# High weights meet both parts of the later tokens in one matmul, with token halves of 280 and 240

## The chip, the cores and the metric

The kernel runs on one core of one Trainium2 chip. The metric is the device time of one launch in microseconds; the kernel before takes 1524.72 us, the median of three runs (1524.21 to 1529.47). Engines by their short names: PE is TensorE (PEld its weight loads), DVE is VectorE, ACT is ScalarE, POOL is GpSimd, SP is SyncE, which issues the DMAs here.

## The reference

One inference step of a two-layer decoder over 512 prompt tokens and 8 sample tokens, all in float32: layer 0 mixes with an S5 state-space block, layer 1 with attention that reads one shared K/V; both also attend to 256 memory tokens; both end in a ConvFFN. What matters here is the part that is linear in the tokens:

```python
h = rmsnorm(x, p['norm_mix_pre'][l]);  z = h @ p['w_in'][l]            # (520, 1024) @ (1024, 1024)
...
o = jnp.concatenate([seq_out, mem_out], axis=-1) @ p['w_out'][l]       # 1024 -> 1024
x = x + rmsnorm(o, p['norm_mix_post'][l])
f, cp = conv_ffn(rmsnorm(x, p['norm_ffn_pre'][l]), ...)
x = x + rmsnorm(f, p['norm_ffn_post'][l])

def conv_ffn(h, w_up, cw, cb, w_down, prev):
    u = h @ w_up                                   # 1024 -> 5632
    y, new_prev = causal_dwconv(u, prev, cw, cb)   # width 3 along the tokens
    g, val = jnp.split(y, 2, axis=-1)
    return (jax.nn.silu(g) * val) @ w_down, new_prev   # 2816 -> 1024
```

Between the layers the shared K, V and log-forget values are made from x by `rmsnorm(s, g) @ w_kv` (1024 to 1548).

## The kernel before

Activations lie transposed: features on the 128 partitions, the NT = 520 tokens (512 of the prompt, 8 samples) along the free axis. A dense product is cut into panels of 128 output features. To keep float32 precision with single-pass float32r matmuls, both operands are split: w = w_hi + w_lo, x = x_hi + x_lo, each part rounded to float32r, and three products are added in PSUM, hi·hi, hi·lo and lo·hi. The tokens are cut into HALF = (0, 264) and (264, 520), each in a PSUM bank of its own. So `product` (L2638) does, for each k of a panel (KD = 8 blocks of 128 input features, KH = 11 for half of the "down" product), six matmuls, three terms times two halves, L2649. The memory keys and values use the same function with one range of 256 columns.

**A panel's way through the engines.** Panel q lies in slot q % 2: one of two weight buffers and two of the four banks of `big`. SP loads the raw weights (`raw`). ACT makes w_hi (L2144), for panel q + 2 once panel q is done (`panel_done`). POOL makes w_lo = raw - w_hi (L949; in some phases DVE does, L1208) and raises `lo_made`. PE waits for `lo_made` and, before it writes a slot's banks again, for `panel_read` of the panel two before (L2640 to L2642). DVE waits for `panel_done`, reads both banks and raises `panel_read` with the second read.

**Who reads.** `read_panel` (L1549) serves w_in of layer 0 and K/V: it multiplies each half by rstd, the token's inverse norm, on the way out of PSUM. The queries of layer 1 are read on L1944 to L1950. w_out and "down" are copied or added into y by `copy_out` (L1776 to L1796), `read_half` (L1762) and the loop at L1857 to L1860. Of the last pair of panels of such a phase PE does the first half of both panels and then the second half of both (`last_pair`, L2704); `first_pair` (L2732) starts a phase in the same way.

**The "up" panels.** The FFN is done in two halves of the hidden width, f = 0 and 1; each has 22 "up" panels (11 pairs: a gate panel and its value panel) and then 8 "down" panels over KH = 11 blocks. With two layers that is 4 phases of 11 laps. DVE's lap is the loop at L1809. For each of the two panels: two reads with the factor rstd into `uc` (L1826 and L1827, the second raises `panel_read`); a wait for ACT's tap, in which ACT first copies the last tokens (`newconv`, L2502, it waits for `panel_read`) and then scales `uc` into `yc` (L2506); then two scalar_tensor_tensor over 512 tokens that add the taps before (L1831, L1836), each with a small one for the 8 samples (L1834, L1837). After the second panel: hf = silu(gate) * value, h_hi and h_lo (L1842 to L1846), which the "down" product takes as its right side. All of these from L1831 on read and write SBUF.

DVE and ACT run their queues in the order written; nothing is scheduled at run time.

Of the kernel before, what the change touches and what calls it, by code (L numbers as in the profile page):

```python
# [21 lines left out]
F32R = mybir.dt.float32r  # L22
# [6 lines left out]
P = 128  # L29
T = 512  # L30
NB = 8
NT = T + NB
HALF = ((0, 264), (264, NT))
# [268 lines left out]
def program(nc, I, O):  # L302
# [4 lines left out]
    with ctx:  # L307
# [63 lines left out]
        x_hi = split("x_hi", [P, KD, NT], F32R)  # L371
        x_lo = split("x_lo", [P, KD, NT], F32R)
# [82 lines left out]
        h_hi = a("h_hi", [P, KH, NT], F32R)  # L455
        h_lo = a("h_lo", [P, KH, NT], F32R)
# [725 lines left out]
        def _(dve):  # L1182
# [366 lines left out]
            def read_panel(q, dst_of, mult=True):  # L1549
# [212 lines left out]
            def read_half(ph, m, n, add):  # L1762
# [7 lines left out]
                ins = V.tensor_tensor(dst, dst, src, add) if add else V.tensor_copy(dst, src)  # L1770
# [5 lines left out]
            def copy_out(ph, add=None, conv=None):  # L1776

                for m in range(6):
                    q = PH[ph][2] + m
                    dve.wait_ge(panel_done, q + 1)  # L1780
                    for n_, (c0, c1) in enumerate(HALF):
                        dst, src = y[:, m, c0:c1], big[2 * (q % 2) + n_][:, 0:c1 - c0]
                        ins = V.tensor_tensor(dst, dst, src, add) if add else V.tensor_copy(dst, src)
                        if n_:
                            tell(ins, panel_read, q + 1)
                        else:
                            do(ins)
# [10 lines left out]
            def ffn(l):  # L1798
                for f in range(2):
                    _, n, base, _ = PH[f"up{l}{f}"]  # L1800
                    step0, r = own.n, None
                    K = 10
# [6 lines left out]
                    with dve.Fori(0, KH) as it:  # L1809
# [6 lines left out]
                        def sy():  # L1816
                            dve.wait_ge(dve_step, it * K + (step0 + c[0]))

                        for half in range(2):
# [6 lines left out]
                            st(V.tensor_tensor(uu[:, 2:266], big[2 * slot][:, 0:264], rstd[:, 0:264], ALU.mult))  # L1826
# [1592 lines left out]
```

## Time and profile before

| | |
|---|---|
| median of three runs | 1524.72 us (1524.21 to 1529.47) |
| span of the profiled execution, first to last instruction | 1519.0 us |
| PE busy | 1413.4 us, 93% |
| PEld busy | 1313.9 us, 86% |
| DVE busy | 976.7 us, 64% |
| POOL busy | 638.5 us, 42% |
| ACT busy | 576.7 us, 38% |
| mean granted TensorE clock | 0.971 |

The page gives the profiled execution no time of its own beside the span; the runs' median is 5.7 us above it. Busy time is the union of an engine's instructions. A matmul's record is longer than the distance to the next one, since matmuls overlap in the array: the cost of one in a stream is the distance between two starts. A row of the timeline gives start, duration, engine, line, operation, out<-in, shapes, and in brackets how long the engine was idle before and what ended that. The chain of work is followed back from the last instruction.

### The profile page before, as it was taken

The numbers are of one execution on the slowest core, as the hardware profiler recorded it, in microseconds if no ns is written. First come the engines' busy times: TensorE is split into PE (matmuls) and PEld (weight loads), VectorE is DVE, ScalarE is ACT, GpSimd is POOL, SyncE is SP. The second block draws the span as 40 slices with busy tenths as digits, with TensorE's granted clock in tenths as the row PEclk, the third lists the DMA queues.
The fourth block names the chain that finished last, engine by engine and source line by source line (L and its number), as shares of the span: only waits on it lengthen the run. The fifth ranks groups of instructions, "written<-read, shape, count | busy, mean of one in ns | idle before, by whom it ended". The sixth has DMA issues, their size and how long they took to land.

```text
span 1519.0 us, 32537 instructions
## 1 busy us (share of the span) xinstructions
PE 1413.4 (93%) x12097; PEld 1313.9 (86%) x12097; DVE 976.7 (64%) x1658; ACT 576.7 (38%) x1019; POOL 638.5 (42%) x420
## 2 busy tenths in 40 slices
PE   6986978989999999999799989999989999999997
PEld 6984758979999999999699966657889999999997
DVE  5769967576773167765748688753677761376755
ACT  4544354344432133422415235432454431234323
POOL 1586422304444334433177888402223443344430
PEclk9998789989999999999999999999999999999999
DMA  5344364213333232332145769995213233233321
GB/s 173 114 117 79 63 169 123 83 44 85 99 94 98 77 97 83 102 98 75 45 121 164 226 175 308 331 340 157 69 57 97 84 103 90 83 91 88 104 83 62
DMA packets 289082, 180.47 MB, mean 119 GB/s; under 512 B 54248, under 2 KB 274572, under 8 KB 288924
## 3 DMA queue, kind: packets, MB, share of 16 engines
q1 hardware_dynamic: 288412, 179.07, 40.9%
q8 instruction: 61, 1.00, 0.3%
q14 instruction: 33, 0.27, 0.1%
q10 hardware_dynamic: 576, 0.13, 0.0%
HBM read 167.10 MB, written 10.63 MB: 117 GB/s over the span
## 4 chain that ended last, share of the span: by engine, by line
PE 70%; DVE 14%; issue 8%; ACT 2%; SPq 2%; DMA 1%; POOL 1%; DVEq 0%; ACTq 0%; POOLq 0%
PE big L2649 58%; PE big L2715 3%; PE misc L2800 2%; DVE tmp L1261 2%; PE big L2746 2%; DVE y L1738 1%; DVE rstd L1219 1%; DVE x L1744 1%; DVE w_lo L1208 1%; DVE x_lo L1251 1%; SPq L597 1%; PE misc L2770 1%; ACT yc L2506 1%; DVE cp L1261 1%; ACT w_hi L2144 1%
## 5 line engine op out<-in xcount | busy, mean ns | idle before, releaser
L949 POOL TENSOR_TENSOR w_lo<-raw,w_hi 128x1024 fp32r<-128x1024 f32 (+2 forms) x153 | 393.8, 2574 | 708.9 <-ACT w_hi L2144 548.4
L2144 ACT ACTIVATE w_hi<-raw 128x1024 fp32r<-128x1024 f32 (+2 forms) x179 | 198.5, 1109 | 582.1 <-PE big L2649 539.0
L2649 PE MATMUL big<-x_hi,w_hi 128*128 128x264 f32 x1984 | 406.7, 287 | 8.4 <-DVE uc L1827 2.8
L2649 PE MATMUL big<-x_hi,w_lo 128*128 128x264 f32 x1984 | 400.8, 283 | 0.0
L2649 PE MATMUL big<-x_lo,w_hi 128*128 128x264 f32 x1984 | 398.8, 283 | 0.0
L2649 PEld LDWEIGHTS big<-x_hi,w_hi 128*128 128x128 f32 x1984 | 305.9, 189 | 13.1 <-issue 4.7
L2649 PEld LDWEIGHTS big<-x_lo,w_hi 128*128 128x128 f32 x1984 | 305.6, 189 | 0.0
L2649 PEld LDWEIGHTS big<-x_hi,w_lo 128*128 128x128 f32 x1984 | 305.3, 189 | 0.0
L1831 DVE SCALAR_TENSOR_TENSOR yc<-uc,convw,yc 128x512 f32<-128x512 f32 x88 | 136.7, 1554 | 113.2 <-ACT yc L2506 113.2
L2649 PE MATMUL big<-h_hi,w_hi 128*128 128x264 f32 x616 | 125.1, 284 | 6.3 <-DVE h_lo L1846 6.3
L2649 PE MATMUL big<-h_hi,w_lo 128*128 128x264 f32 x616 | 123.9, 282 | 0.0
L2649 PE MATMUL big<-h_lo,w_hi 128*128 128x264 f32 x616 | 123.9, 282 | 0.0
L2649 PEld LDWEIGHTS big<-h_hi,w_hi 128*128 128x128 f32 x616 | 94.1, 188 | 7.4 <-DVE h_lo L1846 7.1
L2649 PEld LDWEIGHTS big<-h_lo,w_hi 128*128 128x128 f32 x616 | 94.4, 188 | 0.0
L2649 PEld LDWEIGHTS big<-h_hi,w_lo 128*128 128x128 f32 x616 | 94.4, 188 | 0.0
L1859 DVE COPY y<-big 128x264 f32 (+1 forms) x32 | 12.2, 424 | 102.6 <-PE big L2649 102.6
L1093 POOL TENSOR_TENSOR areas<-areas,qb 128x768 f32<-128x768 f32 x41 | 74.6, 1830 | 7.0 <-DMA areas<-in_cache_k 6.2
L1836 DVE SCALAR_TENSOR_TENSOR yc<-uc,convw,yc 128x512 f32<-128x512 f32 x88 | 66.2, 752 | 12.7 <-DVE yc L1834 0.2
L2506 ACT ACTIVATE yc<-uc,convw 128x520 f32<-128x520 f32 x88 | 72.3, 821 | 1.1
L1201 DVE TENSOR_TENSOR sumsq<-sumsq,sq 128x520 f32<-128x520 f32 x20 | 52.5, 2627 | 11.7 <-ACT sq L2461 9.9
L2746 PE MATMUL big<-x_hi,w_hi 128*128 128x264 f32 (+1 forms) x96 | 38.4, 400 | 17.8 <-DVE x_lo L1251 10.4
L1219 DVE RECIPROCAL rstd<-sd 128x264 f32<-128x264 f32 (+1 forms) x16 | 28.3, 1773 | 31.5 <-ACT sd L2177 31.5
(434 smaller groups left out, 2330.8 us busy)
## 6 DMA issues: line engine op xcount, KB each, us to landing
raw<-in_w_up SPq DMA_DIRECT2D x88, 512.0 KB, 3.9
raw<-in_w_down SPq DMA_DIRECT2D x32, 704.0 KB, 4.7
areas<-in_cache_k SPq DMA_DIRECT2D x41, 384.0 KB, 4.5
areas<-in_cache_v SPq DMA_DIRECT2D x41, 384.0 KB, 4.7
raw<-in_w_in SPq DMA_DIRECT2D x16, 512.0 KB, 4.2
raw<-in_w_out SPq DMA_DIRECT2D x16, 512.0 KB, 4.2
raw<-in_w_kv SPq DMA_DIRECT2D x12, 512.0 KB, 4.6
spare<-in_cache_k SPq DMA_DIRECT2D x12, 384.0 KB, 4.5
```

The lines of the kernel that those rows point to most:

```text
L949: pool.tensor_tensor(w_lo[slot][:, 0:kb, :], raw[slot][:, 0:kb, :], w_hi[slot][:, 0:kb, :].bitcast(F32), ALU.subtract).then_inc(lo_made, 1)
L1093: own.tell(pool.tensor_tensor(p, p, qb[b % 2][:].rearrange("p (a d) -> p a d", a=2), ALU.mult), s_("k_product"), n + 1)
L1201: ins = V.tensor_tensor(sumsq[:], sumsq[:], sq[:, m % 2, :], ALU.add)
L1219: tell(V.reciprocal(rstd[:, c0:c1], sd[:, c0:c1]), s_("rstd_ready"), nstd[0])
L1261: do(V.tensor_tensor(o, a_, b_, op))
L1831: st(V.scalar_tensor_tensor(yy[:, 0:T], uu[:, 1:1 + T], w_[1], yy[:, 0:T], ALU.mult, ALU.add))
L1836: st(V.scalar_tensor_tensor(yy[:, 0:T], uu[:, 0:T], w_[0], yy[:, 0:T], ALU.mult, ALU.add))
L2144: A.activation(w_hi[slot][:, 0:kb, :], raw[slot][:, 0:kb, :], ACT.Copy).then_inc(hi_made, 1)
L2506: A.activation(yy[:], uu[:, 2:2 + NT], ACT.Identity, bias=convw[:, 1 - l, bass.ds(it + (f * KH + half * KF + 132), 1)], scale=convw[:, 1 - ...
L2649: ins = pe.matmul(big[2 * slot + b_][:, 0:c1 - c0], w[slot][:, k, :], r[:, c0:c1], start=(k == 0 and n_ == 0), stop=(k == kb - 1 and n_ == 2))
L2715: return pe.matmul(big[2 * slot + b_][:, 0:c1 - c0], w[slot][:, k, :], r[:, c0:c1], start=(k == 0 and n_ == 0), stop=(k == kb - 1 and n_ = ...
L2746: ins = pe.matmul(big[2 * slot + b_][:, 0:c1 - c0], w[slot][:, k, :], r[:, k, c0:c1], start=(k == 0 and n_ == 0), stop=(k == KD - 1 and n_ ...
```

## The change

The high and low parts of x (and of h) become one tile, x_hl = [P, 2, KD, NT], so that one matmul can stream both parts of the later tokens against w_hi: its moving operand is [P, 2, 240], its output 480 columns of one bank, hi·hi beside hi·lo. The two aren't added by PE, so whoever reads the panel adds them. The matmul w_lo·x_hi of the later tokens adds into the first 240 columns. For each k there are five matmuls: three of 280 columns, one of 480, one of 240.

- `joined` and `term` take the place of `product` in all phases but the memory's and the glu's; `product_by_halves`, `last_pair` and `first_pair` use `term`.
- `both(slot, dst)` is a tensor_reduce on DVE over [P, 240, 2] of PSUM, the two parts side by side in stride, into SBUF.
- `read_panel` and the "up" lap: first `both` into the place of the later tokens, then the read of the first 280 times rstd, then, after a wait for `both`, the later tokens times rstd, in SBUF, in place. This last one raises `panel_read`. The lap counts 12 steps for 10.
- `copy_out` and `read_half`: where the panel is copied, `both` takes the place of the second copy; where it is added to y, two adds take the place of one.
- The queries of layer 1 add first and multiply then, and `panel_read` is raised after the second read of the first bank.
- All fixed numbers 264, 256 and 248 follow HALF.

The core of the diff:

```diff
-HALF = ((0, 264), (264, NT))
+HALF = ((0, 280), (280, NT))
...
-        x_hi = split("x_hi", [P, KD, NT], F32R)
-        x_lo = split("x_lo", [P, KD, NT], F32R)
+        x_hl = split("x_hl", [P, 2, KD, NT], F32R)
+        x_hi, x_lo = x_hl[:, 0], x_hl[:, 1]
...
+            def both(slot, dst):
+
+                src = big[2 * slot + 1][:, 0:2 * LATE].rearrange("p (a t) -> p t a", a=2)
+                return V.tensor_reduce(dst, src, AX.X, ALU.add)
...
                 dve.wait_ge(panel_done, q + 1)
+                do(both(slot, late))
+                added = own.n
                 for n, (c0, c1) in enumerate(HALF):
-                    dst, src, r = dst_of(n, c0, c1), big[2 * slot + n][:, 0:c1 - c0], rstd[:, c0:c1]
+                    dst, src, r = dst_of(n, c0, c1), late if n else big[2 * slot][:, 0:c1 - c0], rstd[:, c0:c1]
+                    if n:
+                        dve.wait_ge(dve_step, added)
...
+                    if add:
+                        do(V.tensor_tensor(late, late, high, ALU.add))
+                        added = own.n
+                        do(V.tensor_tensor(first, first, src, ALU.add))
+                        dve.wait_ge(dve_step, added)
+                        ins = V.tensor_tensor(late, late, low, ALU.add)
+                    else:
+                        do(V.tensor_copy(first, src))
+                        ins = both(q % 2, late)
...
-                            st(V.tensor_tensor(uu[:, 2:266], big[2 * slot][:, 0:264], rstd[:, 0:264], ALU.mult))
-                            V.tensor_tensor(uu[:, 266:2 + NT], big[2 * slot + 1][:, 0:256], rstd[:, 264:NT],
-                                            ALU.mult).then_inc(panel_read, 1)
+                            late = uu[:, 2 + HALF[1][0]:2 + NT]
+                            st(both(slot, late))
+                            st(V.tensor_tensor(uu[:, 2:2 + HALF[0][1]], big[2 * slot][:, 0:HALF[0][1]], rstd[:, 0:HALF[0][1]],
+                                               ALU.mult))
+                            sy(1)
+                            V.tensor_tensor(late, late, rstd[:, HALF[1][0]:NT], ALU.mult).then_inc(panel_read, 1)
...
+            def term(slot, n, k, kb, hl):
+
+                c0, c1 = HALF[0] if n in (0, 2, 3) else HALF[1]
+                o, wide = big[2 * slot + (n in (1, 4))], c1 - c0
+                if n == 1:
+                    return pe.matmul(o[:, 0:2 * wide].rearrange("p (a t) -> p a t", a=2), w_hi[slot][:, k, :],
+                                     hl[:, :, k, c0:c1], start=(k == 0), stop=False)
+                w, part = (w_lo if n > 2 else w_hi), 1 if n == 2 else 0
+                return pe.matmul(o[:, 0:wide], w[slot][:, k, :], hl[:, part, k, c0:c1],
+                                 start=(k == 0 and n == 0), stop=(k == kb - 1 and n > 2))
+
+            def joined(q, slot, kb, hl, wait_k=None, free=True, each=None):
+
+                pe.wait_ge(lo_made, q + 1)
+                if free:
+                    pe.wait_ge(panel_read, q - 1)
+                for k in range(kb):
+                    if wait_k is not None:
+                        wait_k(k)
+                    for n in range(5):
+                        ins = term(slot, n, k, kb, hl)
+                    if k == kb - 1:
+                        ins.then_inc(panel_done, 1)
```

## Rows read from the trace of the kernel before

**Rows 1.** The page: busy time by engine; shares of the chain by line.
```profile
PE 1413.4 (93%) x12097; PEld 1313.9 (86%) x12097; DVE 976.7 (64%) x1658; ACT 576.7 (38%) x1019; POOL 638.5 (42%) x420
...
PE big L2649 58%; PE big L2715 3%; PE misc L2800 2%; DVE tmp L1261 2%; PE big L2746 2%; DVE y L1738 1%; DVE rstd L1219 1%; DVE x L1744 1%; DVE w_lo L1208 1%; DVE x_lo L1251 1%; SPq L597 1%; PE misc L2770 1%; ACT yc L2506 1%; DVE cp L1261 1%; ACT w_hi L2144 1%
```

**Rows 2.** Windows: length, busy PE, PEld, DVE, ACT, POOL; PEclk, DMA share, GB/s.
```profile
346.00:456.00 110.00, 109.72 (x913) 109.52 (x912) 78.30 (x146) 46.35 (x69) 45.71 (x19) 1.00 0.35 96
...
470.00:520.00 50.00, 49.40 (x411) 49.40 (x412) 5.89 (x15) 9.10 (x7) 19.30 (x6) 1.00 0.30 83
...
806.00:890.00 84.00, 83.38 (x662) 79.73 (x660) 63.42 (x97) 25.70 (x33) 75.28 (x37) 1.00 0.66 190
```

**Rows 3.** Timeline of DVE, one lap of two "up" panels.
```profile
376.99 0.42 DVE L1826 TENSOR_TENSOR uc<-big,rstd 128x264 f32<-128x264 f32 x1
377.33 0.41 DVE L1827 TENSOR_TENSOR uc<-big,rstd 128x256 f32<-128x256 f32 x1
379.08 1.10 DVE L1831 SCALAR_TENSOR_TENSOR yc<-uc,convw,yc 128x512 f32<-128x512 f32 x1 [1.34 <-ACT yc L2506]
...
380.46 0.75 DVE L1836 SCALAR_TENSOR_TENSOR yc<-uc,convw,yc 128x512 f32<-128x512 f32 x1
...
381.27 0.42 DVE L1826 TENSOR_TENSOR uc<-big,rstd 128x264 f32<-128x264 f32 x1
...
383.31 1.91 DVE L1831 SCALAR_TENSOR_TENSOR yc<-uc,convw,yc 128x512 f32<-128x512 f32 x1 [1.28 <-ACT yc L2506]
...
385.51 0.75 DVE L1836 SCALAR_TENSOR_TENSOR yc<-uc,convw,yc 128x512 f32<-128x512 f32 x1
...
388.52 0.43 DVE L1826 TENSOR_TENSOR uc<-big,rstd 128x264 f32<-128x264 f32 x1
```

**Rows 4.** Timeline of POOL in that lap.
```profile
377.24 2.39 POOL L949 TENSOR_TENSOR w_lo<-raw,w_hi 128x1024 fp32r<-128x1024 f32 x1 [4.10 <-DVE h_lo L1846]
382.26 2.42 POOL L949 TENSOR_TENSOR w_lo<-raw,w_hi 128x1024 fp32r<-128x1024 f32 x1 [2.63 <-ACT w_hi L2144]
```

**Rows 5.** Timeline of DVE and POOL near the start of the first "up" phase.
```profile
354.94 0.43 DVE L1826 TENSOR_TENSOR uc<-big,rstd 128x264 f32<-128x264 f32 x1
355.20 2.40 POOL L949 TENSOR_TENSOR w_lo<-raw,w_hi 128x1024 fp32r<-128x1024 f32 x1 [4.10 <-DVE h_lo L1846]
...
359.25 0.42 DVE L1826 TENSOR_TENSOR uc<-big,rstd 128x264 f32<-128x264 f32 x1
359.49 2.40 POOL L949 TENSOR_TENSOR w_lo<-raw,w_hi 128x1024 fp32r<-128x1024 f32 x1 [1.89 <-DVE yc L1837]
...
365.73 0.43 DVE L1826 TENSOR_TENSOR uc<-big,rstd 128x264 f32<-128x264 f32 x1
```

**Rows 6.** Timeline of PE in the last pair of "down" panels: 264 columns, then 256.
```profile
711.77 0.29 PE L2715 MATMUL big<-h_hi,w_hi 128*128 128x264 f32 x1
...
715.81 0.28 PE L2715 MATMUL big<-h_hi,w_hi 128*128 128x256 f32 x1
...
719.74 1.47 PE L2715 MATMUL big<-h_hi,w_lo 128*128 128x256 f32 x11
...
723.64 1.47 PE L2715 MATMUL big<-h_hi,w_lo 128*128 128x256 f32 x11
```

**Rows 7.** A row of the chain (plain f32, 256 columns); timeline, two columns.
```profile
53.16 3.46 PE misc L2834 x16
...
1030.00 0.80 PE L3314 MATMUL misc<-rowsel,rstd 128*128 128x2 f32 x6 [0.75 <-DVE rstd L2050]
```

**Rows 8.** Groups of PE with the shapes kept apart: count, busy us, mean ns.
```profile
L2649 PE MATMUL big<-x_hi,w_hi 128*128 128x264 f32 x992 | 288.6, 291 | 8.4 <-DVE uc L1827 2.8 <-DVE qs L1946 2.4 <-DVE x_lo L1249 1.6
...
L2649 PE MATMUL big<-h_hi,w_hi 128*128 128x264 f32 x308 | 88.7, 288 | 6.3 <-DVE h_lo L1846 6.3
```

**Rows 9.** Groups of DVE: reduces of PSUM, mean ns.
```profile
L1487 DVE TENSOR_REDUCE ast<-big 128x1 f32<-128x512 f32 x12 | 8.2, 687 | 2.4 <-PE big L3000 1.9 <-DVE fst L1439 0.4
...
L1487 DVE TENSOR_REDUCE ast<-big 128x1 f32<-128x384 f32 x12 | 6.6, 551 | 3.2 <-PE big L3000 3.1 <-DVE fst L1465 0.2
```

More of the change, by code:

```diff
@@ L1769, in read_half @@
                 dst, src = y[:, m, c0:c1], big[2 * (q % 2) + n][:, 0:c1 - c0]
-                ins = V.tensor_tensor(dst, dst, src, add) if add else V.tensor_copy(dst, src)
+                if n and add:
+                    for i in range(2):
+                        ins = V.tensor_tensor(dst, dst, big[2 * (q % 2) + 1][:, i * LATE:(i + 1) * LATE], ALU.add)
+                        if i == 0:
+                            do(ins)
+                            sync()
+                elif n:
+                    ins = both(q % 2, dst)
+                else:
+                    ins = V.tensor_tensor(dst, dst, src, add) if add else V.tensor_copy(dst, src)
                 if n:
@@ L1780, in copy_out @@
                     dve.wait_ge(panel_done, q + 1)
[L1781 to L1787, printed above, removed]
+                    first, late = (y[:, m, c0:c1] for c0, c1 in HALF)
+                    src = big[2 * (q % 2)][:, 0:HALF[0][1]]
+                    high, low = (big[2 * (q % 2) + 1][:, i * LATE:(i + 1) * LATE] for i in range(2))
+                    if add:
[4 more added lines that the diff above has]
+                        ins = V.tensor_tensor(late, late, low, ALU.add)
+                    else:
+                        do(V.tensor_copy(first, src))
+                        ins = both(q % 2, late)
+                    tell(ins, panel_read, q + 1)
                     for a_ in conv_rows(m) if conv is not None else ():
@@ L2656, in _, with product_by_halves, phase @@
             xs_ = lambda k: (x_hi[:, k, :], x_lo[:, k, :])
[L2658 removed]
+            def product_by_halves(q, slot, kb, hl, wait_half):
                 pe.wait_ge(lo_made, q + 1)
                 pe.wait_ge(panel_read, q - 1)
[L2662 removed]
+                for b_ in range(2):
                     wait_half(b_)
                     for k in range(kb):
[L2665 to L2668 removed]
+                        for n in ((0, 2, 3), (1, 4))[b_]:
+                            ins = term(slot, n, k, kb, hl)
                 ins.then_inc(panel_done, 1)
[L2671 removed]
+            def phase(name, hl=x_hl, wait_k=None, wait_half=None, first=0, last=0):
                 kb, n, base, _ = PH[name]
@@ L2710, in last_pair @@
                         slot = q % 2
-                        def part(k, n_):
-                            xh, xl = rhs(k)
-                            w, r = ((w_hi, xh), (w_hi, xl), (w_lo, xh))[n_]
-                            return pe.matmul(big[2 * slot + b_][:, 0:c1 - c0], w[slot][:, k, :], r[:, c0:c1],
-                                             start=(k == 0 and n_ == 0), stop=(k == kb - 1 and n_ == 2))
                         if b_ == 0:
@@ L2734, in first_pair @@
                 add = x_stats(name)
-                for b_, (c0, c1) in enumerate(HALF):
+                for b_ in range(2):
                     for p_ in range(2):
@@ L2744, in first_pair @@
                                 x_split(KD * b_ + k)
-                            for n_, (w, r) in enumerate(((w_hi, x_hi), (w_hi, x_lo), (w_lo, x_hi))):
-                                ins = pe.matmul(big[2 * slot + b_][:, 0:c1 - c0], w[slot][:, k, :], r[:, k, c0:c1],
-                                                start=(k == 0 and n_ == 0), stop=(k == KD - 1 and n_ == 2))
+                            for n_ in ((0, 2, 3), (1, 4))[b_]:
+                                ins = term(slot, n_, k, KD, x_hl)
                             if b_ == 0 and p_ == 0 and k == LAST_READ:
```

104 lines of the change are left out of this document (55 added, 49 removed).

## The prediction

> **What bounds the kernel now.** The page first: TensorE (PE) is busy 93% of the span, VectorE (DVE) 64%, and 58% of the chain that ended last is the one matmul line L2649 [rows 1]. So the kernel is a PE kernel, and every other engine matters only where PE has to wait for it. The windows say where that could be [rows 2]: in 346 to 456 (the first "up" panels) PE is busy 109.7 of 110 us, but DVE is busy 78.3 of 110; in 470 to 520 ("down" panels) DVE is busy 5.9 of 50; in the K/V panels, 806 to 890, DVE is busy 63.4 of 84 and GpSimd (POOL) 75.3 of 84. The clock is full in all three.
>
> DVE's busy share hides waits in its queue, so I read its timeline of one lap of two "up" panels [rows 3]. The first read of a panel starts at 376.99, that of its partner at 381.27, the next one at 388.52: a lap of 11.53 us, two panels of PE. In it DVE stands idle twice, 1.34 and 1.28 us, for ACT's tap. And the same kind of instruction on L1831 takes 1.10 us in one half and 1.91 in the other, where L1836, of the same shape, takes 0.75. The cause is in POOL's rows [rows 4]. w_lo (L949) starts at 377.24 and 382.26 and ends at 379.63 and 384.68; the two slow instructions end at 380.18 and 385.22, both 0.55 after POOL's end. They don't run slowly, they are held until POOL is done. The read of PSUM at 377.33 lies beside POOL's work and takes 0.41 us: it is not held. What differs is that L1831 has two inputs in SBUF and the read has one. The other way round POOL waits too: 4.10 us until DVE's h_lo is done [rows 4].
>
> A lap is therefore made of DVE's own work, ACT's two answers and POOL's holds, and it just fits. Where DVE is behind (354.94 to 365.73) a lap takes 10.79 [rows 5], so it has 0.74 us in hand.
>
> **The change part by part, on PE.** Per k a panel has six matmuls (three of 264, three of 256 columns) and will have five: three of 280, one of 480, one of 240. The columns stay: 1560. So what is saved is what a matmul costs beside its columns. One stretch with 264 alone takes 33 starts from 711.77 to 715.81, 122.4 ns each; one with 256 takes 33 from 719.74 to 723.64, 118.2 ns [rows 6]. At 2.4 GHz the columns are 110.0 and 106.7 ns; 12 ns are left for each. A k costs 3 x 122.4 + 3 x 118.2 = 722 ns.
>
> For 480 columns I take the nearest long stream: plain f32 matmuls with 256 columns twice through the array, 16 records in 3.46 us, 216 ns for 213 ns of columns [rows 7], 3 ns beside: 203 ns. For 280, 116.7 + 12 = 128.5, lower end 119. For 240: six matmuls with two columns each and a full 128x128 weight load take 0.80 us with 0.25 for the last one's own length (an estimate of 0.11 each) [rows 7], so a load alone sets a floor of some 110; with 12 on the columns 112; I take the 118 of the 256 columns. Sum: 3 x 128.5 + 203 + 118 = 706.5, so 16 ns per k. Ends: 3 x 119 + 202.5 + 111 = 670 (52 ns saved), and, if the stream itself is slow (0.452 ns a column with 2.5 beside, which 122.4 and 118.2 allow too), 718 (4 saved).
>
> The Trainium skill (TensorE: Matmul & The Clock Gate, Back-to-back issue gap) gives N/2.4 + 2.5 ns for a matmul by itself, under which one matmul fewer saves 2.5 ns per k. The trace has 118.2 where it gives 109.2.
>
> L2649 has 992 + 308 k-steps of this form [rows 8], of which the 24 of glu keep it; the last pairs (76 k), the first pairs (48) and the one product by halves (8) add 132, so 1408 change: 704 in "up", 352 in "down", 128 in w_out, 224 in w_in and K/V. Where PE stays the bound all of it would be 1408 x 16 ns = 22.5 us.
>
> **On DVE, in the "up" panels.** Now: two reads of PSUM (next start 0.34 later each). After: `both`, a reduce over 480 elements of PSUM; the read of 280; then, after a wait for `both`, a multiply of the late 240 in place. Reduces of 512 and 384 take 687 and 551 ns [rows 9], 1.06 ns an element, so 480 takes 653, about 0.58 until the next start; 280 columns take 0.36; the multiply about 0.40. The read then ends 1.34 after its start, for 0.75 before: +0.59 per panel. That groups of two are reduced at this rate no row shows; a reduce twice as slow would end at 1.15 and change little, as is seen below.
>
> Without POOL a lap would be: read 1.34, ACT's answer 1.34, L1831 to L1836 1.03, to the next read 0.81 = 4.52; the second half 1.34 + 1.28 + 1.03 + 3.01 = 6.66 [rows 3]. Together 11.18, against PE's 11.53 - 16 x 0.016 = 11.27. That would still fit. But the two holds of 2.4 us have to go somewhere, and the late multiply is the new thing: **it has both inputs in SBUF**, where the old late read had one in PSUM. Behind it wait panel_read (so PE's next product into these banks), ACT's newconv and tap, and through the tap all that DVE does next.
>
> Where do the holds fall? In the laps in which DVE is behind, POOL starts at 355.20 and 359.49, 0.26 and 0.24 after the read's start (354.94, 359.25), in both halves [rows 5]: its weights are ready earlier, DVE's run of SBUF work lets it in only when the PSUM read begins. After the change this is the usual case. POOL runs from 0.25 to 2.65 after the read's start; the late multiply would start at 0.94, is held, and ends 0.2 after POOL (L1831 ended 0.2 sooner than its own 0.75 would say), at 2.85. So a panel's read takes 2.85 for 0.75. The halves become 2.85 + 1.34 + 1.03 + 0.81 = 6.03 and 2.85 + 1.28 + 1.03 + 3.01 = 8.17: **a lap of 14.2 us**, longer than PE's 11.3, so DVE and POOL set it and PE waits for panel_read, some 2.9 us a lap. L1831 is no longer held: that is counted (1.03 is its 0.75 and 0.28 from its end to L1836). Against 11.53 it is +2.67; 44 laps: **+118 us**.
>
> Ends: a hold costs least where it falls wholly into ACT's answer, 2.4 - 1.3 = 1.1 each, lap 13.4, +81 us. If the multiply needs its full 0.40 after POOL, lap 14.6, +135.
>
> The Trainium skill (SBUF — State Buffer, Who interferes with whom) has a rule that speaks against this change: a DVE instruction with two SBUF inputs is locked out for the whole of a GpSimd instruction that reads SBUF, and a tensor_reduce never is. The rows above show the first; no row shows a reduce beside POOL's reads in these panels.
>
> **Elsewhere.** "Down" and w_out panels: DVE has 44 of 50 us free [rows 2], the added reduce or second add (some 0.4 to 0.6 per panel) hides under PE; what it costs if that cover is gone is that same 0.6 a panel. Here PE gains: (352 + 128) x 16 ns = -8 us (ends -2 and -25). At the end of each of the four runs into a norm, one read of a panel is exposed: 4 x 1 = +4. In K/V (12 panels) DVE has 20.6 us free in 84 and POOL is busy 90% [rows 2]: 12 x (0.6 + a mean hold of 0.9) = 18 us eat nearly all of it; +5. w_in of layer 0 and 1 (16 panels) are like it, with DVE's preparation of the S5 tables behind: +5. Ends of both together 0 and +30.
>
> **Sum.** 1519.0 (span) + 118 - 8 + 4 + 10 = 1643; the median of the runs is 1524.7, 5.7 above the profiled span, which lies around it: 1649. I say **1650**. The mechanism's ends: 81 - 25 + 4 = +60 to 135 - 2 + 4 + 30 = +167, so 1585 to 1692.
>
> **The rivals.**
> *PE stays the bound (faster).* If the late multiply is not held, the lap without holds is 11.18 and the old pattern (holds on L1831 and ACT's answer) absorbs the rest; then only PE's saving shows: 1524.7 - 22.5 + 4 = 1506, with its ends 1460 and 1523. For it: a read lies beside POOL unheld. Against it: its source is PSUM; and even at best 2.2 us of holds don't fit into 0.1.
> *Half of it.* POOL falls into the gap of ACT's answer in one half only, or gets in ahead of the hf work: laps of 12.5, +43 - 8 + 14, 1574.
> *Nothing.* Saving and holds cancel, or the slow-stream end (4 ns per k) comes true and the multiply is not held: 1520 to 1530.
> *Narrow matmuls (far slower).* No row has such matmuls (the ones fed from x_hi, w_hi) with under 256 columns. If the chip took 240 as it takes plain f32, in two records of 216 ns for 256 columns [rows 7], one would cost 405 ns for 118, 0.29 us per k: 1408 x 0.29 = +408, and with -22 + 14 beside it 1925 (a lap of 15.9 us then, PE's own). It decides from the first panel on; nothing in the trace speaks for it.
>
> **How the numbers follow.** The forecast's mechanism 0.73; half of it 0.07; PE stays the bound 0.14; nothing 0.04; narrow matmuls 0.02. The predicted time is 1650. The range 1560 to 1720 takes in the first two, 0.80, with some room above for the waits that a slower DVE stretches at the turns from "up" to "down", where PE waits for the last h. Faster by over 0.5% (about what a measurement of this kernel can tell from no change): 0.14. Within: 0.04. Slower: 0.82.
>
> **What would show it.** In the new trace: the late multiply of the "up" panels at about 1.9 us where its 240 elements need 0.4, ending just after POOL's w_lo, and L1831 back at 0.75; laps of 14.2 us; PE busy near 80% there, with idle time put down to DVE uc. The 480-column matmul should start its successor after 203 ns, the 280 after 128, the 240 after 118; "down" panels of 11 k should take 7.7 us for 7.9. I am wrong if the multiply shows 0.4 us beside a running w_lo, if `both` shows far over 0.65, or if POOL starts elsewhere than just behind the read's start.

## The result and the profile after

| | before | after |
|---|---|---|
| median | 1524.47 us (1523.25 to 1529.47) | 1667.87 us (1666.09 to 1668.82) |
| ratio, 95% interval | | 1.0933 (1.0908 to 1.0957), slower |
| span of the profiled execution | 1519.0 us | 1666.9 us |
| PE, DVE busy | 93%, 64% | 88%, 68% |
| mean granted TensorE clock | 0.971 | 0.944 |

The change costs 143 us. The page of the kernel after, busy time and shares of the chain by engine and by line; it answers [rows 1]:

```profile
PE 1463.6 (88%) x10689; PEld 1302.2 (78%) x10689; DVE 1138.4 (68%) x1790; ACT 571.8 (34%) x1019; POOL 640.9 (38%) x420
...
PE 39%; DVE 36%; issue 11%; ACT 6%; DVEq 2%; SPq 2%; DMA 2%; POOL 1%; ACTq 1%; POOLq 0%
PE big L2686 19%; DVE uc L1857 9%; PE big L2683 8%; ACT yc L2546 4%; DVE uc L1554 3%; PE misc L2856 2%; DVE hf L1871 2%; DVE yc L1866 2%; PE big L2715 1%; DVE sc L1961 1%; DVE yc L1863 1%; SPq L597 1%; DVE h_hl L1873 1%; DVE y L1749 1%; DVE tmp L1261 1%
```

1408 matmuls are gone (10689 for 12097). The chain, 58% one PE line before, is shared between PE and DVE, and its first DVE line, L1857, is the late multiply of the "up" laps. The windows (columns as in [rows 2]) over the first "up" panels, the turn with the first "down" panels, and K/V:

```profile
346.00:456.00 110.00, 95.85 (x606) 89.19 (x605) 84.70 (x132) 35.13 (x56) 37.75 (x16) 0.94 0.27 73
470.00:520.00 50.00, 40.58 (x254) 38.05 (x255) 30.33 (x45) 13.68 (x19) 16.71 (x6) 0.93 0.34 87
821.00:905.00 84.00, 73.59 (x488) 68.22 (x486) 66.37 (x93) 26.44 (x34) 61.62 (x30) 0.96 0.43 122
```

PE, full in all three before, is idle 12 to 19% in each, and the granted clock is under 1 in them. The second window holds the end of the "up" phase now, since everything is later.

DVE's timeline of one lap, beside [rows 3]:

```profile
403.74 0.65 DVE L1554 TENSOR_REDUCE uc<-big 128x240 f32<-128x480 f32 x1
404.30 0.44 DVE L1854 TENSOR_TENSOR uc<-big,rstd 128x280 f32<-128x280 f32 x1
404.66 1.95 DVE L1857 TENSOR_TENSOR uc<-uc,rstd 128x240 f32<-128x240 f32 x1
407.94 0.75 DVE L1860 SCALAR_TENSOR_TENSOR yc<-uc,convw,yc 128x512 f32<-128x512 f32 x1 [1.33 <-ACT yc L2546]
...
409.78 0.65 DVE L1554 TENSOR_REDUCE uc<-big 128x240 f32<-128x480 f32 x1
...
410.70 1.97 DVE L1857 TENSOR_TENSOR uc<-uc,rstd 128x240 f32<-128x240 f32 x1
413.95 0.75 DVE L1860 SCALAR_TENSOR_TENSOR yc<-uc,convw,yc 128x512 f32<-128x512 f32 x1 [1.28 <-ACT yc L2546]
...
418.01 0.65 DVE L1554 TENSOR_REDUCE uc<-big 128x240 f32<-128x480 f32 x1
```

POOL's and one row of PE's in it, beside [rows 4]:

```profile
403.99 2.35 POOL L949 TENSOR_TENSOR w_lo<-raw,w_hi 128x1024 fp32r<-128x1024 f32 x1 [5.87 <-DVE h_hl L1875]
406.66 0.40 PE L2686 MATMUL big<-x_hl,w_hi 128*128 128x280 f32 x1 [2.25 <-DVE uc L1857]
410.02 2.39 POOL L949 TENSOR_TENSOR w_lo<-raw,w_hi 128x1024 fp32r<-128x1024 f32 x1 [3.68 <-DVE yc L1866]
```

The halves are 6.04 and 8.23 us, the lap 14.27 (14.4 in the second "up" phase of each layer). POOL starts 0.25 and 0.24 after the read's start; the late multiply takes 1.95 for 240 elements and ends 0.27 after w_lo (406.61, 406.34). PE starts 0.05 later; it had been idle for 2.25. DVE's groups over the whole kernel: L1857 is long, L1860 (the L1831 of before, mean 1554 ns there) isn't any more, and the reduce takes the 0.65 us that was put down for it:

```profile
L1857 DVE TENSOR_TENSOR uc<-uc,rstd 128x240 f32<-128x240 f32 x88 | 151.2, 1718 | 0.0
L1860 DVE SCALAR_TENSOR_TENSOR yc<-uc,convw,yc 128x512 f32<-128x512 f32 x88 | 69.2, 786 | 112.8 <-ACT yc L2546 112.8
...
L1554 DVE TENSOR_REDUCE uc<-big 128x240 f32<-128x480 f32 x88 | 57.3, 651 | 10.4 <-PE big L2686 9.9 <-DVE uc L1831 0.5
```

PE's new matmuls in the last pair of "down" panels, beside [rows 6]:

```profile
780.55 2.98 PE L2686 MATMUL big<-h_hl,w_hi 128*128 128x280 f32 x22
783.37 1.58 PE L2686 MATMUL big<-h_hl,w_lo 128*128 128x280 f32 x11
...
788.63 1.40 PE L2686 MATMUL big<-h_hl,w_lo 128*128 128x240 f32 x11
789.87 2.55 PE L2683 MATMUL big<-h_hl,w_hi 128*128 128x480 f32 x11
792.25 0.95 PE L2686 MATMUL big<-h_hl,w_lo 128*128 128x240 f32 x7
```

By the starts: 280 columns 128.2 ns each, 240 112.7, 480 216.4. A k costs 3 x 128.2 + 216.4 + 112.7 = 713.7 ns for 722: 8 ns saved, not 16. This is the price in the last pair, where each width runs in a row of its own. Over whole panels, where the widths alternate, less is saved: the "down" panels take 7.88 us for 7.92 before (by the starts of their reads, a mean over the phase), 4 ns a k, and not the forecast 7.7.

The same late multiply with POOL idle, in the last lap of the first "up" phase, is the check within this trace: 0.40 us. What POOL's wider w_lo for the "down" weights holds there is hf (views of DVE, POOL and PE):

```profile
487.53 3.55 DVE L1871 TENSOR_TENSOR hf<-sg,yc 128x520 f32<-128x520 f32 x1
...
493.33 0.40 DVE L1857 TENSOR_TENSOR uc<-uc,rstd 128x240 f32<-128x240 f32 x1
...
487.23 3.29 POOL L949 TENSOR_TENSOR w_lo<-raw,w_hi 128x1408 fp32r<-128x1408 f32 x1 [3.28 <-ACT w_hi L2183]
...
493.83 0.39 PE L2686 MATMUL big<-h_hl,w_hi 128*128 128x280 f32 x1 [3.59 <-issue]
```

**Where the 147.9 us of the two spans lie**, by the starts of DVE's reciprocals, which begin and end each norm: to the first norm +4.7; the two FFNs +65.2 and +65.3; w_in, K/V, attention and w_out of layer 1 +12.4; norms and tail +0.3. So 130.5 of it is the FFN, where the laps were forecast to grow.

### The profile page after: what moved, and what is told of

Read it like the earlier page. It is cut to its first block, busy times and chain, and to the rows that moved or that the text cites. A ratio compares the mean times of both kernels' runs of the same rounds, so it can differ in the third digit from the quotient of the medians.

```text
span 1666.9 us, 29941 instructions
## 1 busy us (share of the span) xinstructions
PE 1463.6 (88%) x10689; PEld 1302.2 (78%) x10689; DVE 1138.4 (68%) x1790; ACT 571.8 (34%) x1019; POOL 640.9 (38%) x420
## 4 chain that ended last, share of the span: by engine, by line
PE 39%; DVE 36%; issue 11%; ACT 6%; DVEq 2%; SPq 2%; DMA 2%; POOL 1%; ACTq 1%; POOLq 0%
PE big L2686 19%; DVE uc L1857 9%; PE big L2683 8%; ACT yc L2546 4%; DVE uc L1554 3%; PE misc L2856 2%; DVE hf L1871 2%; DVE yc L1866 2%; PE big L2715 1%; DVE sc L1961 1%; DVE yc L1863 1%; SPq L597 1%; DVE h_hl L1873 1%; DVE y L1749 1%; DVE tmp L1261 1%
## 5 line engine op out<-in xcount | busy, mean ns | idle before, releaser
L2686 PE MATMUL big<-x_hl,w_hi 128*128 128x280 f32 x2112 | 625.9, 306 | 93.8 <-DVE uc L1857 67.4
L2686 PEld LDWEIGHTS big<-x_hl,w_hi 128*128 128x128 f32 x2112 | 403.7, 194 | 115.7 <-DVE uc L1857 82.3
L2686 PE MATMUL big<-x_hl,w_lo 128*128 128x280 f32 (+1 forms) x2112 | 438.7, 287 | 0.0
L2683 PE MATMUL big<-x_hl,w_hi 128*128 128x480 f32 x1056 | 408.0, 392 | 0.0
L2686 PEld LDWEIGHTS big<-x_hl,w_lo 128*128 128x128 f32 x2112 | 345.8, 193 | 30.5
L2686 PE MATMUL big<-h_hl,w_hi 128*128 128x280 f32 x704 | 199.8, 303 | 27.1 <-issue 14.8
L2683 PEld LDWEIGHTS big<-x_hl,w_hi 128*128 128x128 f32 x1056 | 205.6, 195 | 3.3 <-DVE x_hl L1251 0.2
L2686 PEld LDWEIGHTS big<-h_hl,w_hi 128*128 128x128 f32 x704 | 133.8, 197 | 29.0 <-issue 15.5
L1857 DVE TENSOR_TENSOR uc<-uc,rstd 128x240 f32<-128x240 f32 x88 | 151.2, 1718 | 0.0
L1860 DVE SCALAR_TENSOR_TENSOR yc<-uc,convw,yc 128x512 f32<-128x512 f32 x88 | 69.2, 786 | 112.8 <-ACT yc L2546 112.8
L2686 PE MATMUL big<-h_hl,w_lo 128*128 128x280 f32 (+1 forms) x704 | 140.3, 290 | 0.0
L2683 PE MATMUL big<-h_hl,w_hi 128*128 128x480 f32 x352 | 133.1, 396 | 0.0
L1865 DVE SCALAR_TENSOR_TENSOR yc<-uc,convw,yc 128x512 f32<-128x512 f32 x88 | 66.2, 752 | 12.7
L2683 PEld LDWEIGHTS big<-h_hl,w_hi 128*128 128x128 f32 x352 | 69.4, 198 | 1.2
```

The costliest lines, as they stand in the source:

```text
L1857: V.tensor_tensor(late, late, rstd[:, HALF[1][0]:NT], ALU.mult).then_inc(panel_read, 1)
L1860: st(V.scalar_tensor_tensor(yy[:, 0:T], uu[:, 1:1 + T], w_[1], yy[:, 0:T], ALU.mult, ALU.add))
L1865: st(V.scalar_tensor_tensor(yy[:, 0:T], uu[:, 0:T], w_[0], yy[:, 0:T], ALU.mult, ALU.add))
L2683: return pe.matmul(o[:, 0:2 * wide].rearrange("p (a t) -> p a t", a=2), w_hi[slot][:, k, :], hl[:, :, k, c0:c1], start=(k == 0), stop=False)
L2686: return pe.matmul(o[:, 0:wide], w[slot][:, k, :], hl[:, part, k, c0:c1], start=(k == 0 and n == 0), stop=(k == kb - 1 and n > 2))
```

## The experiments

Ratios are to the kernel before, run on the same chip.

**1. The hold alone, without the change.** In the "up" laps of the kernel before:

```diff
+late = uu[:, 266:2 + NT]
+st(V.tensor_copy(late, big[2 * slot + 1][:, 0:256]))
 st(V.tensor_tensor(uu[:, 2:266], big[2 * slot][:, 0:264], rstd[:, 0:264], ALU.mult))
-V.tensor_tensor(uu[:, 266:2 + NT], big[2 * slot + 1][:, 0:256], rstd[:, 264:NT],
-                ALU.mult).then_inc(panel_read, 1)
+sy(1)
+V.tensor_tensor(late, late, rstd[:, 264:NT], ALU.mult).then_inc(panel_read, 1)
```

> The kernel before with one thing altered: in the "up" laps the read of the late 256 tokens is a copy out of PSUM into uc, then comes the read of the first 264, then a wait for the copy and the multiply by rstd in place, both inputs in SBUF; it raises panel_read. PE and everything else are as before, there is no reduce, and what is computed stays the same. Theory (POOL's w_lo holds the multiply that has two SBUF inputs): the multiply lasts about 1.9 us and ends just behind w_lo, the lap is 14.0 to 14.4 us against 11.53, 44 laps give +110 to +125, so 1635 to 1650 us, ratio about 1.077. Rival A (the reduce, or the new shapes of the matmuls, slow the changed kernel's laps): DVE's own lap of about 11.1 still fits, laps stay at 11.5, 1525 us. Rival B (any third step in a read costs its own time only, unheld): two times 0.5 us more in a lap that has 0.74 in hand, laps of 11.8, 1536 us.

Measured: 1651.7 us, 1.084 (1.0816 to 1.0865), 1.7 above the expected range; laps of 14.31. Timeline of DVE, then of POOL:

```profile
396.99 0.42 DVE L1827 COPY uc<-big 128x256 f32<-128x256 f32 x1
...
397.67 2.25 DVE L1830 TENSOR_TENSOR uc<-uc,rstd 128x256 f32<-128x256 f32 x1
...
397.25 2.39 POOL L949 TENSOR_TENSOR w_lo<-raw,w_hi 128x1024 fp32r<-128x1024 f32 x1 [5.86 <-DVE h_lo L1848]
```

With the matmuls, halves and tiles of before and no reduce, a third step in each read, with both inputs in SBUF, brings 126 of the 143 us. Both rivals fall. (Experiment 6 keeps the third step and changes the place of its input alone.) The multiply ends 0.28 after POOL.

**2. Other steps in the changed read.** The reduce last, from SBUF, behind a multiply out of PSUM:

```diff
-st(both(slot, late))
+st(V.tensor_tensor(sq[:, :, 0:LATE],
+                   big[2 * slot + 1][:, 0:2 * LATE].rearrange("p (a t) -> p a t", a=2),
+                   rstd[:, HALF[1][0]:NT].unsqueeze(1).to_broadcast([P, 2, LATE]), ALU.mult))
...
-V.tensor_tensor(late, late, rstd[:, HALF[1][0]:NT], ALU.mult)
+V.tensor_reduce(late, sq[:, :, 0:LATE].rearrange("p a t -> p t a"), AX.X, ALU.add)
```

> The changed kernel; in the "up" laps the late tokens' two steps change places: first a multiply of all 480 columns by rstd, out of PSUM into a spare tile, then the read of the first 280, then, last, the reduce of 2 x 240 from SBUF into uc, which raises panel_read. DVE has as many steps and slightly more elements; what is computed is the same up to rounding. The step behind the wait has one SBUF input in place of two. Theory (the hold needs two SBUF inputs): no step of the read is held, the reduce ends about 0.7 us after its start whether POOL runs or not, the lap is PE's or near it, 11.4 to 11.8 us, the total 1535 to 1560 us. Rival (the laps are long because DVE has more work and a wait more in each read, whatever the inputs are): laps stay at 14.3, 1665 us. Between them: if L1860 and its like are held again as before the change (1.1 to 1.9 us for 0.75), laps of about 12.5 and 1590 us.

Measured: 1579.0 us, 1.0348 (1.0321 to 1.0375). Timeline of DVE, then of POOL:

```profile
403.69 0.65 DVE L1853 TENSOR_TENSOR sq<-big,rstd 128x480 f32<-128x480 f32 x1
404.26 0.44 DVE L1855 TENSOR_TENSOR uc<-big,rstd 128x280 f32<-128x280 f32 x1
404.61 0.67 DVE L1858 TENSOR_REDUCE uc<-sq 128x240 f32<-128x480 f32 x1
...
403.95 2.40 POOL L949 TENSOR_TENSOR w_lo<-raw,w_hi 128x1024 fp32r<-128x1024 f32 x1 [4.55 <-DVE h_hl L1877]
```

A reduce that reads and writes SBUF lasts 0.67 in the middle of w_lo: not held. The laps are 11.71 (11.8 in the second "up" phases), as expected. But the total is 19 us over the upper end: the last lap of each "up" phase takes 17.0 (12.7 before) and the clock falls to 0.78 at the turn. There POOL's wider w_lo, for the "down" weights, gets in ahead of h_lo and of a step over 8 elements:

```profile
461.13 3.42 POOL L949 TENSOR_TENSOR w_lo<-raw,w_hi 128x1408 fp32r<-128x1408 f32 x1 [3.19 <-ACT w_hi L2185]
468.91 3.67 POOL L949 TENSOR_TENSOR w_lo<-raw,w_hi 128x1408 fp32r<-128x1408 f32 x1 [4.35 <-ACT w_hi L2185]
...
461.61 3.50 DVE L1877 TENSOR_TENSOR h_hl<-hf,h_hl 128x520 f32 x1
469.41 3.19 DVE L1868 SCALAR_TENSOR_TENSOR yc<-convs,convw,yc 128x8 f32<-128x8 f32 x1
```

**3. Shorter POOL instructions.**

```diff
-pool.tensor_tensor(w_lo[slot][:, 0:kb, :], ...)
+for a_, b_ in ((0, kb // 2), (kb // 2, kb)):
+    ins = pool.tensor_tensor(w_lo[slot][:, a_:b_, :], ...)
```

> The changed kernel with POOL's w_lo (one subtraction over 1024 elements a partition, 2.35 us) written as two over 512, back to back; nothing else differs and what is computed is the same. Theory (an instruction of DVE with two SBUF inputs is held until the POOL instruction under way ends, and gets in between two): the late multiply of the "up" laps is held until the first of the two ends, about 1.5 us after the read's start, and the second half of w_lo then has to wait for a gap in DVE's work, which ACT's answer of 1.3 us gives; laps of 11.7 to 12.6 us, total 1550 to 1590. Rival (POOL keeps the way to SBUF from its first instruction to its last, or DVE is slowed by the traffic and not by the hold): the multiply still ends 2.85 us after the read's start, lap 14.3, 1668 us.

Measured: 1583.75 us, 1.0392 (1.037 to 1.0414), laps of 12.14. Timeline of DVE, then of POOL:

```profile
399.19 0.65 DVE L1556 TENSOR_REDUCE uc<-big 128x240 f32<-128x480 f32 x1
...
400.12 0.87 DVE L1859 TENSOR_TENSOR uc<-uc,rstd 128x240 f32<-128x240 f32 x1
...
399.44 1.29 POOL L950 TENSOR_TENSOR w_lo<-raw,w_hi 128x512 fp32r<-128x512 f32 x1 [2.28 <-DVE yc L1868]
...
400.68 1.46 POOL L950 TENSOR_TENSOR w_lo<-raw,w_hi 128x512 fp32r<-128x512 f32 x1
```

The multiply takes 0.87 and ends at 400.99, 0.26 after the first of the two POOL instructions (400.73), while the second lasts until 402.14. So DVE gets in between the two, and the hold is that of the one instruction under way. The later phases have laps of 12.2 to 12.3.

**4. "Up" apart.** "Up" back to its old two reads and, by a flag, to six matmuls:

```diff
+if n == 1 and apart:
+    for part in range(2):
+        ins = pe.matmul(o[:, 0:wide], w_hi[slot][:, k, :], hl[:, part, k, c0:c1],
+                        start=(k == 0 and part == 0), stop=False)
+    return ins
```

> The changed kernel with only the "up" panels of the FFN put back to six matmuls per k (three of 280, three of 240 columns) and to their old two reads out of PSUM; the joined matmul and the adds stay in w_in, K/V, w_out, "down" and the queries. What is computed is the same. Theory (all the loss of the FFN is in the "up" laps, and what is lost elsewhere is the 17 us that the segments outside the FFN show): laps of 11.5, the FFN at 374 to 378 us a layer, the total 1524.5 + 17 - 4 = 1535 to 1545. Rival (the "down" panels or the changed order of the first and last pairs carry a part of the FFN's +65 a layer): more than 1555. If the segments' +17 was only a consequence of the late FFN: 1520 to 1527.

Measured: 1536.5 us, 1.0074 (1.0051 to 1.0098), laps of 11.59. As the theory had it: "up" carries 131 of the 143 us, the other stages 11.

**5. Joined only in w_out and "down":** the same flag in w_in, K/V and the queries too, with their old reads.

> Halves of 280 and 240 as in the changed kernel, but the joined matmul and the adds only where DVE has most of its time free: w_out and "down". In "up", w_in, K/V and the queries PE has the six matmuls (three of 280, three of 240 columns) and DVE its old reads. What is computed is the same. Theory (the joined matmul saves PE 9 ns per k wherever nobody waits for DVE, and the whole loss comes from the reads in "up", w_in and K/V): 480 k-steps x 9 ns = 4.3 us saved, laps of 11.59 for 11.53 give back 44 x 0.06 = 2.6, so 1520 to 1525 us against 1525.6. Rival (the +17 us outside the FFN come from w_out, from the added adds there, or from the new halves and not from w_in and K/V): 1535 us, as in the run with only "up" apart.

Measured: 1529.45 us, 1.0025 (1.001 to 1.004). It falls between the two expectations: w_in, K/V and the queries cost 7 of the 11 us, and the rest, 4.6 us, is lost although the change is left only where DVE is free. Not all of that is the joined form's: with the new halves a lap of six matmuls is 11.59 for 11.53, which makes 2.6 us in 44 laps.

**6. The sum kept in PSUM.** The changed kernel with one place altered (`misc` are PSUM banks that are free in this phase):

```diff
-st(both(slot, late))
+hi_ = misc[half][:, 0:LATE]
+st(both(slot, hi_))
...
-V.tensor_tensor(late, late, rstd[:, HALF[1][0]:NT], ALU.mult)
+V.tensor_tensor(late, hi_, rstd[:, HALF[1][0]:NT], ALU.mult)
```

> The changed kernel; in the "up" laps the reduce writes its sum into a free PSUM bank and not into uc, and the late multiply reads it there. DVE has the same three steps of the same lengths with the same wait, and what is computed is the same: only the place of the late multiply's first input differs, PSUM for SBUF. Theory (the hold falls on an instruction with two SBUF inputs): the late multiply takes 0.40 us beside a running w_lo, L1860's like is held again as before the change (1.1 and 1.9), DVE's lap is some 11.2 and PE's 16 x 0.713 = 11.4 becomes the bound, the total 1528 (1536.5 with "up" apart, less 44 x 0.18) to 1545 with the wide w_lo of the turns. Rival (the longer chain reduce, wait, multiply is what costs, with the hold only filling a wait that would be there anyway): laps of 11.7 as with the multiply first, 1579 us, or more.

Measured: 1537.0 us, 1.0076 (1.0047 to 1.0106), laps of 11.43. Timeline of DVE, then of POOL:

```profile
398.59 0.66 DVE L1554 TENSOR_REDUCE misc<-big 128x240 f32<-128x480 f32 x1
399.16 0.44 DVE L1855 TENSOR_TENSOR uc<-big,rstd 128x280 f32<-128x280 f32 x1
399.51 0.40 DVE L1858 TENSOR_TENSOR uc<-misc,rstd 128x240 f32<-128x240 f32 x1
401.19 1.00 DVE L1861 SCALAR_TENSOR_TENSOR yc<-uc,convw,yc 128x512 f32<-128x512 f32 x1 [1.28 <-ACT yc L2547]
...
399.25 2.41 POOL L949 TENSOR_TENSOR w_lo<-raw,w_hi 128x1024 fp32r<-128x1024 f32 x1 [2.50 <-ACT w_hi L2184]
```

The same three steps of the same lengths, and 131 of the 143 us are gone: the multiply takes 0.40 in the middle of w_lo, the hold is back where it was before the change (1.00 for 0.75), behind ACT's answer, and PE's 16 x 0.713 = 11.4 sets the lap.

**7. One piece for two.** The 480 columns of "down" from one contiguous range:

```diff
-hl[:, :, k, c0:c1]
+hl[:, 0, k, 0:2 * wide]
```

> The changed kernel, but in the "down" panels the 480 moving columns are the first 480 tokens of h_hi in one piece and not 2 x 240 out of h_hi and h_lo, which lie 22.9 KB apart in a partition. It leaves the right sums of "down" out; the count and the sizes of all instructions are the same. In the changed kernel 11 starts of the 480 lie 216.4 ns apart, 16.4 ns beside the columns, where those of 240 to 280 have 12. If the two pieces cost the 4 ns, it is 212 here; if it is a matter of the length, 216. The time of the kernel stays within 2 us of 1668 either way.

Measured: 1674.0 us (one execution; 6 over the changed kernel, for an expected 2). The starts of the 480 and of what follows them:

```profile
790.18 2.55 PE L2685 MATMUL big<-h_hl,w_hi 128*128 128x480 f32 x11
792.57 0.61 PE L2689 MATMUL big<-h_hl,w_lo 128*128 128x240 f32 x4
```

217 ns each, as with two pieces. The 4 ns are not the pieces' price. The time is a miss, but of one execution, and nothing is built on it.

**8 and 9. The joined form where it should pay:** "up" with the sum in PSUM, w_out and "down"; first with halves of 280 and 240, then of 264 and 256.

> The joined matmul where it should pay: in "up" with the sum kept in a free PSUM bank, in w_out and in "down"; w_in, K/V and the queries in six matmuls with their old reads. What is computed is the same. Theory: PE's 9 ns per k in 1184 k-steps is 10.7 us, nothing is held that wasn't held before: 1512 to 1518 us against 1525.6, ratio 0.991 to 0.995. Rival (at the turns from "up" to "down" the changed order of POOL and DVE costs more than it did before, as it did with the multiply first, 15 us a layer): 1530 to 1550.

> As the run that joins in "up" (sum in a free PSUM bank), w_out and "down" only, but with the old halves of 264 and 256, so that the joined matmul has 512 columns, a whole bank, in 2 x 256. What is computed is the same. With 280 and 240 this form took 1524.84 us, no better than the kernel before, though its "up" laps were 11.43 for 11.53: the segment from w_in to the last w_out of layer 1 took 342.0 us for 334.5. Theory (the new halves cost something there that the joined matmul doesn't): per k 3 x 122.4 + (213.3 + 16.4) + 118.2 = 715 ns, laps of 11.44, that segment back at 335 to 337, the total 1517 to 1520. Rival (the segment is longer for another reason, the tile x_hl or the clock): 342 again, 1524 to 1526. If 512 columns cost more than the columns and 16 ns, laps of 11.5 and over.

Measured: 1524.84 us, 0.9992 (0.9977 to 1.0008), and 1524.81 us, 0.9989 (0.9972 to 1.0006); laps of 11.43 and 11.44 for 11.53. Neither can be told from the kernel before: two misses, for expected gains of 7 to 14 and of 5 to 8 us. The steady laps are 0.1 us shorter, that is 6 ns a k, and the "down" panels 4 ns a k (experiment 8) and 6 (9), by their reads as above. Over the 1184 k-steps, with w_out put down like "down" (an estimate), PE saves 6 to 7 us and not 10.7. And the first "up" phase of each layer starts 0.5 to 0.7 us later (10.8 and 10.95 us from the norm to the first hf, for 10.25), and its first two laps, in which DVE was behind before, are longer (11.29 and 11.43 in experiment 8, for 10.78 and 11.26). From the norm to the eleventh hf it is 126.1 and 126.4 us for 125.8. That DVE's longer read costs this is argued, not tested. A whole FFN is 0.8 and 1.1 us shorter, 375.9 and 375.6 for 376.7. The 512 columns take 232 ns, 2 more than I had put.

**10. The same halves without "up"** (as 5, with 264 and 256):

```diff
-HALF = ((0, 280), (280, NT))
+HALF = ((0, 264), (264, 520))
```

> As the run that joins in w_out and "down" only (1529.45 us, 4.6 above the kernel before), but with the old halves of 264 and 256. Only 480 k-steps differ from the kernel before, and the tile x_hl. What is computed is the same. If the new halves cost the 4.6 us: 480 x 7 ns = 3.4 us under the kernel before, 1520 to 1523. If it is the joined matmul or its adds in w_out and "down": 1528 to 1530 again.

Measured: 1524.8 us, 0.9995 (0.9977 to 1.0013): between the two. The new halves have part of experiment 5's loss (a lap of six matmuls is 11.59, and 11.51 here), and the expected gain of 3.4 isn't seen.

**11 and 12. Two more tests of the hold,** w_lo in two for "down" on top of 9 (the loop of 3, for `kb > KD` alone and cut at 6 of 11), and the multiply first (2) with all of w_lo in two (3).

> As the run before last of this call (old halves, joined in "up" with the sum in a free PSUM bank, in w_out and in "down"), with POOL's w_lo of the "down" weights, 1408 elements and 3.2 us, written as two of 768 and 640. What is computed is the same. Theory (a hold ends with the POOL instruction under way): the holds of the laps in which "down" weights are split (up to 3.5 us on one DVE instruction) fall to half, the last lap of each "up" phase gets 0.5 to 1 us shorter, four such laps and the start of "down" give 2 to 5 us in all. Rival ("down" hides it, PE has work there): no difference, within 1 us.

> The changed kernel with the multiply first (1579.0 us) and with all of POOL's w_lo in two instructions (1583.8 us alone). What is computed is the same up to rounding. In the run with the multiply first DVE's own work set laps of 11.71, and the last lap of each "up" phase took 17.0 us, because the 3.4 us w_lo of the "down" weights got in ahead of h_lo and of the last small step. Theory (each such hold lasts as long as POOL's instruction): the steady laps stay at 11.7 or rise to 11.8, the last laps fall to 14 to 15 us, the clock after the turn stays higher, the total 1565 to 1573. Rival (the last lap is long for the weights' DMA or ACT, not for the hold): 17 us again, 1579. If the two halves let POOL in more often (two grabs in place of one): laps of 12.1 as with w_lo in two alone, 1590.

Measured: 1526.2 us, 1.0008 (0.9992 to 1.0024), and 1560.6 us, 1.0232 (1.0201 to 1.0264). The first is a miss: last laps of 12.79 for the 12.65 of experiment 9, and 1.4 us more in all. The held instruction arrives some 2 us after POOL's start, so it meets the second half, and waits for that. In the second, h_lo is held to 1.8 us where it was 3.5, the last laps are 13.7 and 15.4 for 17.0 and 17.2, the laps stay at 11.71, and 18 us come back, 4 more than the expected range allows.

## Why the prediction was right, and what it mis-sized

**One sum explains five kernels.** The prediction's lap without holds is 8.50 us (answers 1.34 + 1.28, steps 1.03 twice, 0.81 and 3.01) and twice the read of a panel, or PE's time if that is longer:

| | read, start to end | 8.50 + 2 x read | PE | lap measured |
|---|---|---|---|---|
| after | 2.87 | 14.24 | 11.4 | 14.27 |
| hold alone (1) | 2.93 | 14.36 | 11.53 | 14.31 |
| w_lo in two (3) | 1.80 | 12.10 | 11.4 | 12.14 |
| multiply first (2) | 1.59 | 11.68 | 11.4 | 11.71 |
| sum in PSUM (6) | 1.32 | 11.14 | 11.4 | 11.43 |

The mechanism, its place and size stood as forecast: the read at 2.87 (2.85), POOL's start 0.25 behind it, halves 6.04 and 8.23 (6.03, 8.17), L1860 freed. I had taken the start of POOL from the laps in which DVE is behind [rows 5], and that was the step that mattered: had I kept the pattern of the steady laps [rows 4], one half would have come out cheaper.

The late multiply's 1.95 us beside w_lo agree with the rule of the Trainium skill (SBUF — State Buffer, Who interferes with whom), and so does the reduce: two SBUF inputs are locked out, a reduce isn't. Experiment 2 shows the reduce at 0.67 beside w_lo, which no row of before could, and experiment 3 that the lock is given up between two POOL instructions.

**Where the other 24 us of span are** (forecast 1643, measured 1666.9). All three groups of terms came out above the forecast, so no error of one hides that of another; in the median of the runs 5 of the 24 us don't show, by the last point:

- *Laps and start of the "up" phases,* 22 x 2.67 = 58.7 us a layer forecast, 62.2 measured: +7 in all. The last laps took 16.6 (one of the four 13.8, behind one of 17.5), where the 12.7 of before and 2.67 make 15.4, since the w_lo for "down" is 3.3 us long and falls on hf or on a small step; I had priced every hold at 2.4.
- *The turns and "down",* forecast -2.8 a layer, measured +3.1: +12 in all. The saving was 4 ns a k over whole panels and not 16, which is 2 of the 6 us a layer, and I had put nothing on the turn. PE waits there twice. It starts the first "down" panel at 493.83, after 3.59 us that the profile puts down to nothing; but the late multiply that frees the banks ends 0.10 earlier (493.73), and 0.10 earlier again in the second phase (717.28 and 717.38): what put it off is hf, held for 3.55. This wait lies in the last lap, counted above. Then PE waits 3.50 us for the last h, and behind that, in all four turns and in none of before, the granted clock is at 1.2 GHz for a while. At the first turn it is from 507.7 to 511.1, and there the first two reads of "down" lie 9.45 apart in place of 7.94. The window with this stretch has 0.81 for 1.00:

```profile
508.00:516.00 8.00, 8.00 (x48) 7.62 (x48) 0.42 (x1) 0.68 (x1) 3.21 (x1) 0.81 0.33 92
```

- *Elsewhere,* forecast -2 for w_out, +4 for the norms and +10 for K/V and w_in, that is +12; measured +17: +5. The segment of w_in, K/V and attention in layer 1 was 346.9 us here and, with the same code, 350.0 to 353.5 in the profiles of experiments 2, 6 and 7, so this term is known to some 7 us only. The hold on K/V's in-place multiply was sized well, 1.3 us for 0.4:

```profile
L1569 DVE TENSOR_TENSOR kvT<-kvT,rstd 128x240 f32<-128x240 f32 x11 | 14.2, 1295 | 0.0
```

- *From the span to the run,* 5.7 us forecast. The median lies 1.0 above the span (1667.87). 1.9 lie outside the span (1668.82 against 1666.9 in the profiled execution). The rest was spread between executions: the profiled one of before was among the short ones.

**PE's prices.** 280 was right (128.2 for 128.5). 480 was set too low (203, measured 216): I took it from a plain f32 stream with 3 ns beside the columns [rows 7], but the stream fed from float32r tiles has 12 at 240 to 280 columns and 16 at 480, in one piece as in two. 240 was set too high (118, measured 113). The step that made the saving itself too large lies beside these prices: I took 722 ns from the last pair, where each width runs in a row, for all panels. By the laps and the "down" panels a k of six matmuls costs 720 to 721 ns in whole panels, and one of five 714 in "up" and 716 in "down". The rival of narrow matmuls falls: 240 columns cost less than 256. The Trainium skill (TensorE: Matmul & The Clock Gate, Back-to-back issue gap) gives 2.5 ns beside N/2.4 for a matmul by itself; these streams, with 11 to 18 ns beside the columns, don't show that at any of the widths.

**The rival "PE stays the bound"** forecast 1506 for a late multiply that isn't held. Experiment 6 makes just that kernel: its laps are PE's, as the rival said, and the total is 1537. Its step "only PE's saving shows" fails: w_in, K/V and the queries in the joined form cost 12 us (experiment 6 against 8; 7 by 4 against 5), and in the forms that avoid this (8 and 9) no gain is left that can be measured. The saving was 6 to 7 us to begin with, the first "up" phases take a part of it, and by the clocks another part is given back (below); what else there is isn't settled.

## What to carry to other kernels

When a step gets a second input in SBUF, or its input moves from PSUM to SBUF, look for what GpSimd runs at that moment: the step then costs the rest of GpSimd's instruction, and its place in the queue decides who waits with it. If such a step can't be avoided, keep one input in PSUM, use a reduce, put it where the engine waits for another anyway, or cut GpSimd's instruction so that the step meets a short one.

A matmul fewer saves only what it costs beside its columns, 4 to 6 ns a k here over whole panels, 0.1 us in a lap of 11.5; the later start and the longer first laps of a phase take that back. Measure the price of an instruction in the mix in which it will run: streams of one width promised 8.

## What I had not expected of the hardware

**The price beside the columns grows with the width,** 11 to 13 ns at 240 to 280 columns, 16 to 17 at 480, 18 at 512. A price per column a little over 1/2.4 ns (0.433 between 240 and 480) fits as well.

**The spread of the runs goes with the clock.** Over 59 executions of the kernel before, the span runs from 1518 to 1529 us with a mean granted clock from 0.973 down to 0.963; a line through them gives 0.88 us for 0.001 of clock and accounts for about two thirds of the variance. The twelve executions of experiment 9 have a mean clock of 0.9642 for 0.9667: at equal clock they are 3.1 us shorter, and 2.2 of that is given back. In all four kernels with "up" joined and its hold away the mean clock is 0.963 to 0.966, with "up" apart 0.966 to 0.968. Why is open; a single pair of profiles, as the segments above compare, can mislead by several us for this reason.

**GpSimd's grab can hold a tiny step.** A scalar_tensor_tensor over 8 elements took 3.19 us in experiment 2, and as long in the changed kernel, at 496.54, where the median of its line is 0.22.
